# Moving gathered pairs of a PEER layer from the third dense tile's choices into the query visits

## What is computed

```python
qry = jnp.einsum('cd,dq->cq', xc, w_query).reshape(PEER_CHUNK, PK_HEADS, 2, PK_HALF)
sc = jnp.einsum('chpd,hpnd->chpn', qry, sub_keys)        # 8 heads, 2 halves, 128 keys
s_top, i_top = lax.top_k(sc, PK_TOPK)                    # 16 of each half
cand = s_top[:, :, 0, :, None] + s_top[:, :, 1, None, :] # 256 candidates
best_s, pos = lax.top_k(cand, PK_TOPK)                   # 16 experts of a head
g = jax.nn.softmax(best_s, axis=-1)
act = jax.nn.gelu(jnp.einsum('chkd,cd->chk', expert_u[idx], xc), approximate=False)
out = jnp.einsum('chk,chkd->cd', g * act, expert_v[idx])
```

## Time and profile before

| what | value |
| --- | --- |
| median of 3 runs | 4585.46 us (4581.51 to 4603.41) |
| the profiled execution's own time | 4589.69 us |
| its span, first to last instruction | 4587.9 us |
| mean granted TensorE clock | 0.942 of full |
| expert phase of the 1024-token group | about 2050 us to the end |
| steps start | 2191.7 us |
| the turn of tile 5 (end of the query visits) | about 2477 us |
| the turn of tile 6 (end of the choice stage) | about 2719 us |

### The profile page before, as it was taken

How to read it: one execution, slowest core, us unless ns; L and a number is a source line. 1 busy time by engine, 2 the same in 40 slices (tenths; PEclk the granted TensorE clock), 3 DMA queues, 4 the chain that set the end, 5 groups by cost and what they waited for, 6 DMA issues and landing times.

```text
span 4587.9 us, 61700 instructions
## 1 busy us (share of the span) xinstructions
PE 3973.8 (87%) x22629; PEld 2042.4 (45%) x22629; DVE 2810.5 (61%) x6794; ACT 1275.5 (28%) x3556; POOL 1256.6 (27%) x1018
## 2 busy tenths in 40 slices
PE   7776599998799989997993677779999899999998
PEld 3454444443577764444441344433434343344443
DVE  1332856776888876663878877645555555555544
ACT  0221111221455551112233455522121221122122
POOL 0200232221534413320232232222333222332331
PEclk9888799999899999998995789889999999999999
DMA  6243398886544348756698899999999899999997
GB/s 240 76 180 120 110 364 318 335 354 233 208 176 183 143 167 341 296 227 238 260 347 325 329 396 377 357 366 374 396 411 409 347 407 369 399 402 385 391 403 300
DMA packets 353597, 1383.03 MB, mean 301 GB/s; under 512 B 27152, under 2 KB 112784, under 8 KB 233872
## 3 DMA queue, kind: packets, MB, share of 16 engines
q0 software_dynamic: 129024, 939.58, 51.5%
q1 hardware_dynamic: 162992, 395.47, 23.1%
q10 hardware_dynamic: 61280, 44.04, 2.9%
HBM read 1283.52 MB, written 95.47 MB: 301 GB/s over the span
## 4 chain that ended last, share of the span: by engine, by line
PE 29%; DMA 9%; DVE 9%; issue 4%; ACT 3%; POOL 1%; ACTq 0%; SPq 0%; DVEq 0%; POOLq 0%
PE prompt_exp_wk L2425 10%; PE prompt_exp_wk L2409 10%; DMA prompt_exp_ring<-in_experts_dram,prompt_exp_idx 7%; PE prompt_exp_acc L2387 5%; PE prompt_exp_wk L2333 3%; DVE prompt_exp_junk L2244 3%; DMA gates_dram<-prompt_exp_area 2%; ACT prompt_exp_diag L2069 1%; ACT prompt_exp_wgt L2062 1%; POOL prompt_exp_ring L1963 1%; DVE prompt_exp_hit L2188 1%; DVE prompt_exp_topi L2139 1%; DVE prompt_exp_hT L2232 1%; DVE prompt_exp_top L2136 0%; PE prompt_exp_wk L2372 0%
## 5 line engine op out<-in xcount | busy, mean ns | idle before, releaser
L1963 POOL DMA_INDIRECT prompt_exp_ring<-in_experts_dram,prompt_exp_idx x640 | 698.8, 1092 | 1809.3 <-PE prompt_exp_acc L2387 1605.0
L2244 DVE CUSTOM_DVE_ANT_0 prompt_exp_junk<-prompt_exp_ring,prompt_exp_h 128x1024 bf16<-128x1024 f32 x640 | 762.0, 1222 | 239.7 <-DMA prompt_exp_ring<-in_experts_dram,prompt_exp_idx 225.9
L2425 PE MATMUL prompt_exp_wk<-prompt_exp_area 128*128 128x512 f32 x1536 | 706.2, 607 | 6.5 <-DVE prompt_exp_area L2272 6.5
L2409 PE MATMUL prompt_exp_wk<-prompt_exp_hT,prompt_exp_area 128*128 128x384 f32 x2048 | 702.7, 497 | 0.0
L2387 PE MATMUL prompt_exp_acc<-prompt_exp_ring,prompt_exp_diag 32*32 32x512 f32 x10240 | 392.5, 640 | 267.8 <-ACT prompt_exp_diag L2069 267.7
L537 PE MATMUL prompt_proj_acc<-normed_w,normed_hT 128*128 128x512 f32 x1280 | 553.6, 595 | 14.5 <-PEq L91 14.5
L2409 PEld LDWEIGHTS prompt_exp_wk<-prompt_exp_hT,prompt_exp_area 128*128 128x128 f32 x2048 | 387.3, 193 | 343.9 <-issue 111.0
L152 POOL DMA_INDIRECT sample_hid_ring<-in_experts_dram,sample_hid_idx x256 | 278.8, 1089 | 893.8 <-DVE sample_hid_acc L182 844.3
L2425 PEld LDWEIGHTS prompt_exp_wk<-prompt_exp_area 128*128 128x128 f32 x1536 | 282.2, 191 | 432.7 <-issue 385.8
L2282 DVE TENSOR_TENSOR prompt_exp_area<-prompt_exp_area,prompt_exp_wk 128x512 f32<-128x512 f32 x186 | 127.7, 687 | 519.0 <-PE prompt_exp_wk L2425 495.5
L2055 ACT ACTIVATE prompt_exp_ge<-prompt_exp_dot 128x2 f32<-128x2 f32 x320 | 65.0, 203 | 1241.6 <-DVE prompt_exp_dot L2244 1240.2
(11 more groups left out here) (363 smaller groups left out, 4987.8 us busy)
## 6 DMA issues: line engine op xcount, KB each, us to landing
prompt_exp_area<-in_u_turned_dram SPq DMA_DIRECT2D x128, 512.0 KB, 8.4
prompt_exp_area<-in_experts_dram SPq DMA_DIRECT2D x64, 1024.0 KB, 13.3
gates_dram<-prompt_exp_area ACTq DMA_DIRECT2D x12, 2048.0 KB, 29.2
prompt_exp_area<-gates_dram SPq DMA_DIRECT2D x32, 768.0 KB, 14.6
sample_proj_w<-in_w_all_dram SPq DMA_DIRECT2D x10, 2048.0 KB, 13.9
normed_w<-in_w_all_dram SPq DMA_DIRECT2D x10, 2048.0 KB, 15.2
proj_dram<-prompt_proj_stage SPq DMA_DIRECT2D x80, 256.0 KB, 5.4
prompt_exp_ring<-in_experts_dram,prompt_exp_idx POOLq DMA_INDIRECT x640, 10.1
```

Of the source, the lines that this page charges most:

```text
L1963: nc.gpsimd.indirect_dma_start(out=ring[:, s % RING, :], out_offset=None, in_=experts, in_offset=bass.IndirectOffsetOnAxis(ap=idx[:, n % 2 ...
L2244: nc.vector.tensor_tensor_reduce(out=junk[:, s % 2, :], in0=ring[:, s % RING, 0:D], in1=h2[:, n % 2, :], scale=1.0, scalar=0.0, op0=ALU.mu ...
L2409: last = nc.tensor.matmul(wk[:, j % 2, 0:TURNED], ut[:, j % 3, k, :], hT_dense[:, k, :], start=(k == 0), stop=(k == KD - 1))
L2425: last = nc.tensor.matmul(wk[:, 2 + o % 2, :], act_e[:, c % 2, j, t * P:(t + 1) * P], vt[:, half, j, :], start=(j == 0), stop=(j == JB - 1))
```

## The change

Two arguments in `Turns.walk`:

```diff
@@ in the loop over the query visits
             if v >= 12:
-                self.advance(1 + v % 2)
+                self.advance(2)
@@ in the loop over the third dense tile's choices, twice for each k
                 self.advance(1)
                 if k >= 2:
                     unit_ahead()
-                self.advance(1)
+                self.advance(1 if k % 8 == 7 else 0)
```

## The result

The changed kernel takes 4625.5 us (median of 4 runs, 4622.4 to 4630.0), the kernel before 4588.0 in the runs beside it (4 runs, 4581.5 to 4603.4): a ratio of 1.0075, interval 1.006 to 1.009. The forecast was 4584 with a range to 4614, so it is wrong: the change makes the kernel slower, by about 35 us (0.6 to 0.9% of 4588 is 28 to 41). The profiled execution has a span of 4623.5 us against 4587.9.

The account below looks back on a forecast made before the run. The prediction saw no idle resource to win outright: TensorE, VectorE and DMA limits lay close, differing by stage. Terms 40 + 23 - 69 + 4 = -2 us gave 4587.7 us profiled, 4584 median, range 4559 to 4614.

Parts of the forecast that it names:

- Counting and prices: Steps per stage replayed; a pair priced at 2.30 us on VectorE, 1.14 on TensorE, 5.3 on DMA.
- Query stage, +40: Visits 12 to 31: ten more steps, DMA's rate setting 12.2 us a full visit; +40 us (30 to 59).
- Rival (a): Query stage: the ring's latency bounds a visit at 14.05 us, stage +68, total 4611 us; chance 0.20.
- Tail, +23: Visits 32 to 37, after the last query: VectorE bound, four choices and three pairs added; +23 us (19 to 26).
- Clock, rival (c): Query stage: queries with gaps before them fall to TensorE's lower clock level, +30 us more, total 4614; chance 0.05.
- Choice stage, -69: Choice stage: 14 pairs and four choices leave, 242 us falls to 173 (ends 157 and 185); -69 us (-57 to -85).
- The four choices that move: Tile 1's choices move from the choice stage into the tail, 19.5 us of VectorE work added there and removed here.
- Block stretches, 0: The two block stretches, tiles 6 and 7: steps unchanged, shifted by one in tile 1; 0 us (-3 to 3).
- Dense stream, +4: Dense stream: one pair more, 1.1 us if TensorE sets the pace, 5.3 if DMA does; +4 us (1 to 6).
- that rule: By the skill's 358 GB/s, the query stage's 91 MB take 254 us, ending some 15 us slower, near 4600; chance 0.02.
- (b): Choice stage falls to VectorE's 157 us, -85, query stage to 30 or so above; total 4556 us; chance 0.24.

Follow-up runs that it names:

- later_choices: The changed kernel with tile 1's first choices an octet later in the order, so two go back behind the last queries' pairs; 4615.2 us, ratio 1.0049.
- acts_on_sp: The changed kernel with the eight stores of the dense activations issued on SyncE's queue instead of ScalarE's; 4627.4 us, ratio 1.0055.
- small_gathers_choice: The changed kernel with the gathers awaited in the choice stage fetching half rows, so its output differs; 4612.4 us (one run).
- half_choice: Against the kernel before, only the choice-stage half of the change: one step per half iteration there, query visits as before; 4585.4 us, ratio 0.9989.
- half_query: Against the kernel before, only the query half of the change: two steps in every visit from 12 on, choice stage keeps its second steps; 4635.1 us, ratio 1.009.

## Why the prediction was wrong, step by step

**Counting and prices** held, but for one slip: ten pairs are 20 gathers, and the trace has 20 more in the query stage (74 for 54), where the lower end of that term was worked out with 24; with 20 it would have been +19, not +30. The stages have the steps and choices that the replay gave (a fifth choice falls into the tail because VectorE is later there); VectorE's work in the choice stage came out at 149 us for 157, in the tail at 89 (63 + 26.4).

**Query stage, +40: +45.7.** Right in mechanism and inside its 30 to 59. I took 12.2 us for a visit, it is 12.6 over visits 22 to 31, at a share of 0.93, where I said 0.95. The 5.7 us too little lie elsewhere, though: the visits 16 to 20 with their decodes grew by 13.9 us (61.8 to 75.7), twice the 6.9 that I gave them as VectorE's own time, with 9.9 us of waits for rows there in place of 2.8; the other fifteen grew by 32, where I had 33. And the prediction's opening, that the change moves transfers into a stretch with room, misread the digits: the visits without a decode ran at a share of 0.94 already. Half a pair more a visit took them from 9.9 to 12.6 us, 5.4 for a pair, which is its transfer.

```profile
2304.00:2393.00 89.00, 87.11 (x656) 40.41 (x640) 67.41 (x261) 28.04 (x87) 31.86 (x28) 1.00 0.94 354
```

The idle before dots rose by 22 us where I had thought that it would cover the added dots, but VectorE isn't the limit there and nothing hangs on it. Rival (a) is out: no loop of 14 us.

**Tail, +23: +24.6.** Right in size. That VectorE's work alone sets it isn't borne out: with two choices (9.7 us) out of it, it is 4 us shorter (later_choices).

**Clock, rival (c).** In part. The query stage's granted clock fell from 0.98 to 0.91. TensorE's queries 12 to 31 take 149.1 us for 145.2, and a step's 32 matmuls 51.5 / 37 = 1.39 us for 33.0 / 27 = 1.22; the waits for a diagonal rose from 12.6 to 35.4 us:

```profile
L2387 PE MATMUL prompt_exp_acc<-prompt_exp_ring,prompt_exp_diag 32*32 32x512 f32 x1184 | 51.5, 722 | 35.4 <-ACT prompt_exp_diag L2069 35.4
```

That is 4 + 6 = 10 us of TensorE, a third of what (c) feared, and some of it lies under the waits for rows. I had put it at nothing.

**Choice stage, -69: -50.3.** This is the step that failed, a term of the right sign, mis-sized by 19 us, and outside its own ends (-57 to -85). I set VectorE's 157 against DMA's 149, added half iterations as if only these two could be late, and gave k = 2, 4 and 5 some 18 us each; they took 21.7, 27.1 and 19.9. TensorE was put at nothing in this term, and the order in which the two engines hand over to each other with it. VectorE's idle, to be under 20, is 42 us as before (before 242 less 201, after 191 less 149): its waits for rows went (33.3 to 10.3 us), and in their place came waits of the builds for TensorE. The lines that answer to the earlier trace rows:

```profile
L2244 DVE CUSTOM_DVE_ANT_0 prompt_exp_junk<-prompt_exp_ring,prompt_exp_h 128x1024 bf16<-128x1024 f32 x38 | 45.1, 1220 | 10.3 <-DMA prompt_exp_ring<-in_experts_dram,prompt_exp_idx 7.7 <-issue 2.3 <-DVE prompt_exp_gd L2210 0.3
L2232 DVE TENSOR_SCALAR prompt_exp_hT<-prompt_exp_iota,prompt_exp_ijgT 128x128 f32<-128x128 f32 x128 | 34.6, 348 | 25.6 <-PE prompt_exp_wk L2372 25.3
```

The working had no row of TensorE's order in this stage (block, step, unit, 9.1 us a half) and none of ScalarE's queue. Of the 18 us above my 173, the runs attribute 4 to the store (acts_on_sp) and about 3 to transfers (small_gathers_choice, once its shorter stall is taken off). Some 8 are what the sum of the larger engine per half gives above 173 (181.0 in after); the half with the turn of tile 0 (15.7 us in acts_on_sp, where those around it have 9.1) lies in it, and no run takes that half out alone. The rest I haven't separated.

**The four choices that move** belong to the same step. I charged them at 19.5 us in the tail, which was right, and credited the same 19.5 in the choice stage, where VectorE is the late engine in a few halves only. There they give next to nothing (later_choices).

**Block stretches, 0: +13.2.** Not foreseen and not explained. With the edit of the choice stage tiles 6 and 7 together take 287 to 306 us (eleven kernels), without it 286 to 293 (three). The two overlap, so it isn't shown that the change makes them longer; how much of the 13 us is scatter between profiles stays open.

**Dense stream, +4: +3.2.** Right. Its share of 0.98 at 392 GB/s, and 394 in half_choice, is again above the rate in the Trainium skill ("DMA: Bandwidth & Descriptors", Specifications, about 358 GB/s for a core); the query stage moved 337 GB/s over its length and 365 over visits 22 to 31. The change came out slower, as by that rule, but not for its reason: the query stage took the 254 us that I had worked out by it, but for 86 MB and not 91, and 35 us were lost and not 15.

**The range.** (b) was given 0.24 for a choice stage limited by VectorE alone; nothing that made that stage longer than 173 had a chance of its own, though the term's own end of 185 was in the text. Two engines that hand over to each other in a fixed order deserved a rival on the slow side.

## What to carry over

When two limits lie close together in a stage with a fixed order of instructions, don't take the larger of the two sums: write each engine's time for every half iteration, TensorE's in-order sequence too, and add up the larger of them. Here that comes within 5 us where neither transfers nor a store's issue are late too. Work on an engine that waits for others anyway costs little there, and gives little back when it is taken out: price each move at both ends, by what is late there. Read the share of the DMA engines where the work will go, and not as the mean of a stage. Look at what stands behind a store on the queue of an engine that computes.

## What the runs showed of the hardware

The issue of a store can block the engine that issues it. A 0.8 MB store behind a 2 MB store on ScalarE's queue took 11.1 us to issue in after, 16.9 in before, 10.3 and 6.8 in half_choice and 14.0 in half_query, where the median is 0.34; with the same stores on SyncE's queue the longest took 0.76 us and 0.43 us. It doesn't happen each time: later_choices had 1.3 at most, and the next store in after, 5.6 us behind its 2 MB store, took 0.34. What decides isn't shown. A 2 MB store left on ScalarE's queue still took 8.4 us to issue in acts_on_sp (at 2933 us). The Trainium skill ("DMA: Bandwidth & Descriptors", Issuing engines are not separate DMA queues) says that issuing on several engines only saves the sequencer's time to start a transfer, "which is usually small relative to the DMA itself"; here the store landed 17.6 us after its issue began, and 11.1 of these were the issue. So the statement holds here for the median issue, and not for the longest.

A step of the gathered work takes 1.15 us or 2.02, and which of the two goes with the granted clock. In after's query stage 16 steps followed a wait; the nine at a granted clock of 0.50 to 0.53 took 2.02 us for their 32 matmuls, the seven at 1.00 took 1.15. The length of the wait before doesn't tell them apart (0.27 us came before a long one, 3.95 before a short one). In before two of seven were long. One of each, from TensorE's timeline of after:

```profile
2400.99 2.02 PE L2387 MATMUL prompt_exp_acc<-prompt_exp_ring,prompt_exp_diag 32*32 32x512 f32 x32 [3.82 <-ACT prompt_exp_diag L2069]
...
2425.63 1.15 PE L2387 MATMUL prompt_exp_acc<-prompt_exp_ring,prompt_exp_diag 32*32 32x512 f32 x32 [1.75 <-ACT prompt_exp_diag L2069]
```
